# Decoder trunk on one core: block 1's 22 projection weight pieces in a row at the head of its mixer, its first two state space inputs behind them

## The reference

```python
for layer in range(DEPTH):
    hn = rms_norm(h, norm1_g[layer])
    proj = hn @ w_in[layer]
    qkv_a, z_a, a_a, b_a, u_s, q_c, k_c, v_c = jnp.split(proj, split_at, axis=-1)
    o_a = gdn_mixer(qkv_a, z_a, a_a, b_a, ...)      # gated delta rule, gates from a and b
    o_b = s5_mixer(u_s, ...)                        # state space: a scan over the tokens
    o_c = diff_attn_mixer(q_c, k_c, v_c, ...)       # causal differential attention
    h = h + jnp.concatenate([o_a, o_b, o_c], axis=-1) @ w_out[layer]
    h = h + peer_ffn(rms_norm(h, norm2_g[layer]), peer_wq[layer], peer_keys[layer], peer_u[layer], peer_v[layer])
return rms_norm(h, final_g)
```

## Time and profile before

| | |
|---|---|
| median of 3 runs | 1597.25 us (1595.52 to 1602.94) |
| profiled execution | span 1598.7 us, 17642 instructions; no time of its own beside the span is listed for it |
| VectorE busy | 1109.4 us (69%) |
| GpSimd busy | 992.1 us (62%) |
| TensorE matmul busy | 978.4 us (61%) |
| ScalarE busy | 292.0 us (18%) |
| moved by DMA | 626.50 MB, of which 536.94 MB gathers (q0) and 88.45 MB loads (q1) |

### The profile page before, as it was taken

The page is one execution under the profiler, slowest core; times in us unless marked ns, Lnnn a source line. Parts: engine busy times, 40 slices in busy tenths (PEclk is TensorE's granted clock), DMA queues, the critical chain, the costliest instruction groups (busy, mean ns, idle before and its releaser), DMA issues.

```text
span 1598.7 us, 17642 instructions
## 1 busy us (share of the span) xinstructions
PE 978.4 (61%) x5838; PEld 548.3 (34%) x5838; DVE 1109.4 (69%) x2868; ACT 292.0 (18%) x830; POOL 992.1 (62%) x1031
## 2 busy tenths in 40 slices
PE   9986785866724368886734357978864433333335
PEld 7865663532500045653410025745350000000001
DVE  5948989784657988786476766887557767676440
ACT  5343321331100041232100023324110000000000
POOL 0004666776666776667657775655767777777773
PEclk9998898988855579998876677988785555566658
DMA  9527999999999999999999999997999999999997
GB/s 377 201 90 257 395 379 419 419 419 419 419 419 420 401 403 419 418 418 416 419 420 419 420 419 419 406 420 308 418 419 419 419 419 420 419 419 419 420 418 309
DMA packets 172322, 626.50 MB, mean 392 GB/s; under 512 B 19140, under 2 KB 19140, under 8 KB 172232
## 3 DMA queue, kind: packets, MB, share of 16 engines
q0 software_dynamic: 147456, 536.94, 82.9%
q1 hardware_dynamic: 24776, 88.45, 14.2%
HBM read 624.26 MB, written 1.05 MB: 391 GB/s over the span
## 4 chain that ended last, share of the span: by engine, by line
DMA 29%; DVE 23%; POOL 20%; PE 12%; issue 9%; DVEq 4%; ACT 2%; ACTq 0%; SPq 0%; POOLq 0%
DMA uring<-in_u_tab,small 23%; PE ps L589 12%; DVE uring L1750 10%; POOL uring L2556 7%; POOL vring L2556 7%; DMA gd<-in_u_tab,small 3%; POOL gd L2556 2%; DMA vring<-in_v_tab,small 2%; POOL wring L2556 1%; DMA uring<-in_v_tab,small 1%; DMA sa<-in_u_tab,small 1%; DMA rows<-in_rows 1%; DVE sel L1714 1%; DVE sel L1710 1%; DVE small L1718 1%
## 5 line engine op out<-in xcount | busy, mean ns | idle before, releaser
L1750 DVE CUSTOM_DVE_ANT_0 uring<-uring,ps 128x1024 f32<-128x1024 f32 x462 | 558.3, 1217 | 281.7 <-DMA uring<-in_u_tab,small 261.2
L2556 POOL DMA_INDIRECT uring<-in_u_tab,small x462 | 453.3, 981 | 384.4 <-DVE small L1750 166.0
L589 PE MATMUL ps<-vring,wmat 128*32 128x512 f32 x1748 | 317.9, 848 | 368.1 <-DMA vring<-in_v_tab,small 318.0
L2556 POOL DMA_INDIRECT vring<-in_v_tab,small x437 | 417.3, 955 | 162.4 <-issue 128.1
L589 PEld LDWEIGHTS ps<-vring,wmat 128*32 128x32 f32 x1748 | 57.7, 136 | 554.1 <-DMA vring<-in_v_tab,small 383.0
L589 PE MATMUL ps<-hnT,wring 128*128 128x128 f32 x1200 | 153.4, 286 | 4.0 <-ACT hn L2064 2.1
L589 PEld LDWEIGHTS ps<-hnT,wring 128*128 128x128 f32 x1200 | 144.2, 199 | 30.2 <-issue 21.9
L589 PE MATMUL ps<-wring,hnT 128*128 128x512 f32 (+1 forms) x200 | 87.0, 582 | 13.5 <-DMA wring<-in_w_blocks 12.1
L2546 ACT ACTIVATE small<-small 128x32 f32<-128x32 f32 x16 | 3.7, 230 | 456.4 <-DVEq L1759 456.4
L589 PE MATMUL ps<-gd 128*128 128x128 f32 (+1 forms) x508 | 72.0, 294 | 13.3 <-ACT gd L2064 11.4
L589 PEld LDWEIGHTS ps<-gd 128*128 128x128 f32 x508 | 65.1, 201 | 31.2 <-ACT gd L2064 16.0
(11 more groups left out here) (434 smaller groups left out, 1512.6 us busy)
## 6 DMA issues: line engine op xcount, KB each, us to landing
wring<-in_w_blocks SPq DMA_DIRECT2D x120, 512.0 KB, 7.2
vring<-in_w_blocks SPq DMA_DIRECT2D x32, 512.0 KB, 10.2
uring<-in_u_tab,small POOLq DMA_INDIRECT x462, 13.4
vring<-in_v_tab,small POOLq DMA_INDIRECT x437, 12.1
wring<-in_cols SPq DMA_DIRECT2D x3, 512.0 KB, 6.5
h<-in_x SPq DMA_DIRECT2D x2, 512.0 KB, 9.2
keysT<-in_keys SPq DMA_DIRECT2D x2, 512.0 KB, 13.6
rows<-in_rows SPq DMA_DIRECT2D x2, 486.0 KB, 10.5
```

The lines of the kernel that those rows point to most:

```text
L589: return nc.tensor.matmul(o, a, b, start=start, stop=True, skip_group_check=True)
L1750: V.tensor_tensor_reduce(row_, row_, xp, 1.0, 0.0, ALU.mult, ALU.add, dots[:, j:j + 1]).then_inc(dot_done.sem, 1)
L2556: nc.gpsimd.indirect_dma_start(dst, None, table, bass.IndirectOffsetOnAxis(ap=index, axis=0)).then_inc(done.sem, 16)
```

## The change

Block 1 gets a list of its own for the input projection on TensorE and on ScalarE (`second_projections`). All 22 pieces are multiplied in a row: u, the gate columns, qkv, z, v, q, then the sums of the gates, then k, and only then the first two state space inputs. The v and k products go to PSUM bank 2 and q to bank 3, which the values of the experts use from pair 1 on; so the first `values` waits for the copy of k. `mix` becomes `projections` (blocks 2 and 3, as before) or `second_projections`, followed by `blended`, in which v, q and k are filled for i > 1 only. The norm of block 1 moves into the end of the first mixer: its square and root stand between the scores of wq0 and wq1, the reciprocal between the top results of the first two heads, the scaled copy behind the scores of wq2. SyncE's and GpSimd's lists are unchanged.

```diff
+        def second_projections():
+            V_OUT, Q_OUT, K_OUT = bank(2), bank(3), bank(2)
+            pe.wait_ge(*hn1_ready(1, 1))
+            pe.wait_ge(s0_ready.sem, 5)
+            turn_mix((M0, M1))
+            pe.wait_ge(*trT_ready(1, 1))
+            fill(1, "u", 0, M2, True)
+            pe.wait_ge(*trT_ready(1, 2))
+            fill(1, "u", 1, M2, True)
...
+            ins.then_inc(u_done.sem, 1)
+            for c in range(4):
+                fill(1, f"qkv{c // 2}", c % 2, M0[:, 256 * (c // 2):256 * (c // 2) + 256], c == 0)
+            for half in range(2):
+                fill(1, "qkv2", half, M1[:, 0:256], True)
+            for half in range(2):
+                fill_tokens(1, "z", half, M1[:, 256:512], False)
+            for half in range(2):
+                fill_wide(1, ("v0", "v1"), half, V_OUT, half == 0)
+            for c in range(4):
+                fill(1, f"q{c // 2}", c % 2, Q_OUT[:, 256 * (c // 2):256 * (c // 2) + 256], c == 0)
+            yield 19.5
+            pe.wait_ge(*gbc_ready(1, 1))
+            pe.wait_ge(*fill_act(1, 2))
+            gates_sum()
+            yield 20
+            pe.wait_ge(*fill_act(1, 4))
+            for c in range(4):
+                fill(1, f"k{c // 2}", c % 2, K_OUT[:, 256 * (c // 2):256 * (c // 2) + 256], c == 0)
+            pe.wait_ge(*fill_act(1, 1))
+            bu(1, 0)
+            pe.wait_ge(*bu_ready(1, 1))
+            bu(1, 1)
...
                 if n > 0 and j % 4 == 1:
+                    if n == 1 and j == 1:
+                        pe.wait_ge(*fill_act(1, 6))
```

VectorE:

```diff
-            yield place(i, 34)
-            norm1(i)
+            if i > 1:
+                yield place(i, 34)
+                norm1(i)
...
-            for h0 in range(2):
-                for _ in top(0, h0, 1):
-                    pass
+            for _ in top(0, 0, 1):
+                pass
+            norm1(1)
+            for _ in top(0, 1, 1):
+                pass
```

ScalarE:

```diff
+        def second_projections():
+            turned_scaled(1)
+            softmax(0)
+            yield 3
+            inputs_copy(1)
...
+            yield 14
+            act.wait_ge(*chunk_done(1, AT["v1", 1] + 1))
+            copy(vbuf[:, 1, :], bank(2)).then_inc(fill_act.sem, 1)
+            yield 16.7
+            gate_parts(1)
+            yield 18.5
+            act.wait_ge(*chunk_done(1, AT["q1", 1] + 1))
+            copy(qT[:, :, :], heads4(bank(3))).then_inc(fill_act.sem, 1)
+            yield 19.9
+            gates_spread(1)
+            yield 23.5
+            act.wait_ge(*chunk_done(1, AT["k1", 1] + 1))
+            copy(kT[:, :, P:2 * P], heads4(bank(2))).then_inc(fill_act.sem, 1)
+            yield 23.7
+            bu_copy(1, 0)
+            bu_copy(1, 1)
+            yield place(1, 47.6)
+            decays(1)
...
+            act.wait_ge(x_in[1].sem, 16)
+            act.wait_ge(xp_ready.sem, 1)
+            norm_square(1, hn[:, :]).then_inc(sd_ready.sem, 1)
             for b in range(1, 4):
...
+                if b == 2:
+                    act.wait_ge(*rstd_ready(1, 1))
+                    copy(hn[:, :], h[:, 1, :], rstd).then_inc(hn1_ready.sem, 1)
...
-            softmax(0)
```

More of the change, by code:

```diff
@@ L1038, in mix @@
             bu(i, 3)
-            for half in range(2):
-                yield place(i, 56 + half)
-                fill(i, "q1", half, M3[:, 256:512], False)
+            if i > 1:
+                for half in range(2):
+                    yield place(i, 56 + half)
+                    fill(i, "q1", half, M3[:, 256:512], False)
             yield place(i, 58.5)
@@ L2139, in mix, with turned_scaled @@
                 tables_sin(i)
+            if i == 1:
+                yield from second_projections()
+            else:
+                yield from projections(i)
+            yield from blended(i)
+        def turned_scaled(i):
+            for b, o in enumerate((M0, M1)):
+                act.wait_ge(*tr_done(i, b + 1))
+                for k in range(4):
+                    copy(hnT[:, 4 * b + k, :], o[:, k * P:(k + 1) * P], col("g1")[:, 4 * b + k:4 * b + k + 1])
+                S.drain().then_inc(trT_ready.sem, 1)
@@ new lines, in inputs_copy, with conv_diagonals, gate_parts @@
+        def inputs_copy(i):
+            act.wait_ge(*u_done(i, 1))
+            copy(uT[:, :, :], M2[:, 0:256].rearrange("p (c t) -> p c t", c=2))
+            copy(ab, M2[:, 256:264])
+            S.drain().then_inc(fill_act.sem, 1)
+        def conv_diagonals(n0):
+            for n in range(n0, n0 + 8):
+                ins = copy(convm[:, n, :], ident, col("conv")[:, n:n + 1])
+            if n0 == 16:
+                S.drain().then_inc(convm_ready.sem, 1)
+        def gate_parts(i):
+            act.wait_ge(*a_pre(i, 1))
+            S.activation(beta, ab[:, 4:8], ACT.Tanh, scale=0.5)
+            S.activation(gb_, gb_, ACT.Exp, scale=-1.0)
+            S.activation(ea, row("alog"), ACT.Exp)
+            S.drain()
+            S.activation(gb_, gb_, ACT.Ln, bias=1.0)
+            S.drain().then_inc(a_ln.sem, 1)
@@ new lines, in gates_spread, with decays @@
+        def gates_spread(i):
+            act.wait_ge(*g_ready(i, 1))
+            copy(gbc, bc(gg[:, :, None], [P, HEADS, P])).then_inc(gbc_ready.sem, 1)
+        def decays(i):
+            act.wait_ge(*ngc_ready(i, 1))
+            for hd in range(HEADS):
+                S.activation(dec[:, hd, :], M3[:, hd * P:(hd + 1) * P], ACT.Exp,
+                             bias=ngc[:, hd:hd + 1])
+            S.activation(eg, ngc, ACT.Exp, scale=-1.0)
+            S.drain().then_inc(dec_ready.sem, 1)
@@ L2152, in mix @@
                 act.wait_ge(*params_in(layer, 64))
[L2153 to L2157, removed]
+            turned_scaled(i)
             yield place(i, 40)
[L2159 to L2162, removed]
+            inputs_copy(i)
             for part in range(3):
                 yield place(i, 41 + 0.6 * part)
[L2165 to L2167 removed]
+                conv_diagonals(8 * part)
             yield place(i, 42.6)
```

138 lines of the change are left out of this document (81 added, 57 removed).

## The result

The changed kernel takes 1613.91 us (median of 4 runs, 1608.45 to 1615.03) against 1597.02 us in the comparison beside it: a ratio of 1.0097 [1.0079, 1.0114], **15.5 us slower**. The prediction said 1602.8, in a range of 1595 to 1612: the first time lies outside the range, the second just inside. The intervals in us are wide: 12.6 to 18.2 for the first comparison, 11.0 to 18.2 for the second.

The account below looks back on a forecast made before the run. It took VectorE to bound the kernel from 140 to about 320 us and transfers after that. A 13.3 us wait, less 2.2 and 5.6, left 5.5 us over the median 1597.25: 1602.8 us, range 1595 to 1612.

Parts of the forecast that it names:

- The earlier start of TensorE: Block 1's turns begin at about 144 us instead of 156.38, hidden behind VectorE's own work; worth 0.
- The wait of 13.3 us: VectorE's first state space product in block 1 waits for ScalarE's input copy, now behind all 22 pieces; 13.3 us.
- the q pieces end at about 185.4: TensorE finishes block 1's q pieces at about 185.4 us, after v's second pair of matmuls ends at 177.1.
- a piece land every 2.5 us from 161.3 us on: Block 1's weight loads share the DMA engines evenly with the gathers, so a 0.52 MB piece lands every 2.5 us.
- The wait for TensorE of 2.2 us goes: VectorE's only later wait for TensorE disappears, as v, q and k are gone from 207 us on; 2.2 us off.
- 5.6 us are absorbed: At 321 us, transfers queued ahead keep the DMA engines busy while GpSimd issues late; 5.6 of 11.1 us vanish.
- nothing back here: Weight pieces loaded early give no credit at 321 us, since the kernel before has issued all of them by then too.
- A, holes filled: Early start and twelve pieces brought forward fill up to 10.2 us of transfer holes; 1587 us, chance 0.08.
- B, absorbed by later waits: VectorE's two later waits, for TensorE and gathers, shrink by 4 to 5 us; 1598 us, chance 0.13.
- C, half clock: TensorE does k, and part of v and q, at 1.2 GHz; +7.7 us, 1610.5 us, chance 0.15.
- D, starved dots: Weight loads slow the gathers from 161 to 186 us, VectorE reaches its gates 5 us late; 1608 us, chance 0.13.
- the chain's passing at 366 us: Sign of being right: the chain that ended last passes from VectorE's side to GpSimd's gathers later than 321 us.

Follow-up runs that it names:

- e5_half_loads_third: The changed kernel with only the first half of each of block 1's pieces 10 to 21 loaded; 1607.75 us, ratio 1.0057 to the kernel before.
- e6_warm_third: The changed kernel with six dummy matmuls on TensorE, four ahead of v and two ahead of q; 1607.11 us, ratio 1.0065 to the kernel before.
- e1_inputs_early: The changed kernel with both state space inputs and their copies back at their old places; 1599.86 us, ratio 1.0017 to the kernel before.

## Why the prediction was wrong

The sum was 13.3 - 2.2 - 5.6 = 5.5 us. By its own steps:

- *The earlier start of TensorE: hidden, worth 0.* Right. Alone it gives 0.9997 [0.9987, 1.0006].
- *The wait of 13.3 us.* The mechanism and the place were right, the size was not: 19.8 us (the product at 206.91 for 187.12). The chain from the gates was right in its lengths: sums, four k pieces, input and copy took 195.01 to 206.88, 11.9 us, where the prediction had 13.5, since the sums ran at full clock, 2.1 us for 4.0 (the prediction's own "may save 2"). But this chain did not start from the gates. It started behind q, and *"the q pieces end at about 185.4"* was the **step that failed**: they ended at 193.8, so the sums began 8.1 us later than summed. Of the 8.4 us, 4.1 lie before the end of v (181.2 for 177.1) and 4.3 between v and q, whose first loads were issued at 177.82, when the first v pair was done. In landings: the last v piece came at 176.7 us for 173.5, the first q piece at 184.2 for 176.0. Within q a piece landed every 2.5 us, as summed; the hole of 7.5 us between v and q was not in the sum.
- *Why q was late.* The sum let a piece land every 2.5 us from 161.3 us on, as if the queue of weights were always full. But pieces 15 and later need a slot that v holds, and v comes behind a wait of 5.05 us, which also cost clock. The loads got 34.0% of the DMA engines, not 51%. By the time of the copy, e5_half_loads_third prices the size of the loads at 3.7 us and e6_warm_third the clock in v at 1.8 us; the two can overlap. I put what remains down to the ring's turnover, which wasn't taken away by itself.
- *The wait for TensorE of 2.2 us goes.* Right: between 207 and 268 us the lateness falls from 19.8 to 17.35.
- *5.6 us are absorbed.* Near in size, wrong in its reason. In the traces 4.5 of 17.35 us are gone at 611 us (3.7 of 16.7 in the second profile). But the earlier trace rows's longer landing time is no store of work that a late VectorE can live on: of the delays put in by hand, 11.5 and 20.7 us at 268, nothing was gone at 611 us. What gives back goes with the early loads, the very term of which the prediction said that it gives "nothing back here". That the size came near was luck.

With the measured wait and what the traces show as absorbed the sum is 19.8 - 2.4 - 4.5 = 12.9 us, for 5.5: of the 7.4 us that it was short, 6.3 are the wait (less the 2.4 us that go) and 1.1 the absorption. The total of 15.5 us has 2.6 us more, which no stage of the traces accounts for and which lie within the interval. Without them the time would have been near 1610, inside the range and still 7 us from the forecast.

**The rivals.** A, holes filled: not so; slices 6 to 8 lost more than slice 5 won. B, absorbed by later waits: only so far that VectorE's waits for rows shrink by 4.3 us, and that is the credit the forecast had taken already, not a further one. C, half clock, was priced at 7.7 us for k: k ran at 1.00, 5.52 us for three pieces and 2.05 for the last. The Trainium skill's rule ("TensorE: Matmul & The Clock Gate", "HAM oscillation — how this bites in real kernels") agrees with the trace for v (0.57 after 5.05 us of waiting). The pieces of q and k, behind waits of 3.02, 0.42 to 0.49 and 1.20 us, stayed at 1.00, so the prediction carried the rule too far with its 15.4 us for k. The idle 4.57 us before the sums in the earlier trace rows are 1.20 now. D, starved dots: no wait for a row before the product. In e1_inputs_early VectorE waits for rows three times after it, 3.9 us in all, for the 5 that D was priced at; that the long wait of the changed kernel hides it would fit.

Of what was said to show it right, the turns at 143.57, the rates below 419 between 210 and 290 us and the chain's passing at 366 us came; the wait of 12 to 15 us and loads done by 186 did not. Among what was said to show it wrong, the text did not name a wait well over 15 us. The range ended at 1612 because it took C and D singly. A wait with two starting points, VectorE's gates and the end of q, deserved a case in which the other one leads.

## What to carry to other kernels

When a step is put at the end of a row of loads, work out both chains that end in it, that of the data and that of the ring's slots: a load's start is the end of the use that frees its slot, plus its landing time with the other queue full. While an engine paces the gathers, count a delay of it in full until a run shows that it is absorbed; a long queue further down is no credit. To see what a change costs, add up the transfer time lost up to the place where the transfers take over; here that gave the lateness to 1.3 us in nine profiles. Two small operations that the pacing engine needs soon should stay at the front, even where the row around them moves: here they made 9 of 12.9 us by the traces, and some 13 of 15.5 by the totals. And put milestones of the traces beside the totals: a total from four runs was some 3 us off here.

## What the hardware showed

- A TensorE that waited 5.05 us for a load (4.71 in the second profile) had a mean granted clock of 0.57 (0.69) from 172 to 177 us; six dummy matmuls in the gaps kept it at 1.00. Gaps of 0.42 to 3.02 us between pieces left it at 1.00.
- With both queues in use between 161 and 190 us, the gathers took 68.1% and the weights 34.0%, and the landing time of a gather rose to 14.6 us. In the earlier trace rows it is 51.3% and 51.0%. The Trainium skill ("DMA: Bandwidth & Descriptors", "Queues, rings and completion order") has the engines take turns between queues; the even split of the earlier trace rows agrees. I read the 34% as a queue of weights that is empty part of the time, since SyncE issues no load between 168 and 177 us while it waits for slots.
- Two chips ran the kernel before 9% slower, 1748 to 1750 us for 1597, with gaps of about 1 us between TensorE's instructions that the profile puts down to nothing.
